# Scores first: a new order of the attention and retention work inside each slot of a hybrid decoder layer

## The reference

```
u = rms_norm(x, norm_gain);  z = u @ w_in
q_a,k_a,v_a,g_a, q_i,k_i,w_i, q_r,k_r,v_r,g_r = split(z)
# A) attention, 8 heads x 64, sparse
score[t,s] = sum_h w_i[t,h] * relu(q_i[t,h] . k_i[s]),  causal
each query keeps its 128 best keys;  p = softmax(q_a . k_a / 8 over those keys)
y_a = (p @ v_a) * silu(g_a)
# B) retention, 4 heads, qk 64, v 128, chunks of 128 tokens
S = (q_r k_r^T) * decay;  out = S @ v_r + (q_r * xi) @ state
state = state * g_chunk + (k_r * zeta)^T @ v_r
y_r = rms_norm_per_head(out) * silu(g_r)
h = x + concat(y_a, y_r) @ w_out;   result = rms_norm(h, final_gain)
```

## Time and profile before

| | us |
|---|---|
| median of 3 runs | 291.82 (291.4 to 291.87) |
| the profiled execution | 291.78 |
| its span, first to last instruction | 290.0 |
| PE busy | 280.5 |
| DVE busy | 203.1 |
| ACT busy | 142.2 |
| POOL busy | 65.5 |

### The profile page before, as it was taken

How to read it: one execution, slowest core, us unless ns; L and a number is a source line. 1 busy time by engine, 2 the same in 40 slices (tenths; PEclk the granted TensorE clock), 3 DMA queues, 4 the chain that set the end, 5 groups by cost and what they waited for, 6 DMA issues and landing times.

```text
span 290.0 us, 4405 instructions
## 1 busy us (share of the span) xinstructions
PE 280.5 (97%) x1506; PEld 239.6 (83%) x1506; DVE 203.1 (70%) x418; ACT 142.2 (49%) x303; POOL 65.5 (23%) x121
## 2 busy tenths in 40 slices
PE   7999999999999999999999999999999999999992
PEld 7996778888888788887888888888888888888892
DVE  4866779999999999999946554658635634853342
ACT  5757637525545314584368442592534662351231
POOL 1026812142200068856400103012020020000111
PEclk9999999999999999999999999999999999999998
DMA  7998404211422043152204220212200407301113
GB/s 262 407 399 299 146 3 129 82 23 60 145 73 75 4 148 88 52 145 75 75 6 138 75 72 0 84 63 73 76 0 2 145 0 241 123 36 36 75 72 146
DMA packets 13989, 30.10 MB, mean 104 GB/s; under 512 B 1168, under 2 KB 1680, under 8 KB 13968
## 3 DMA queue, kind: packets, MB, share of 16 engines
q1 hardware_dynamic: 13392, 29.04, 30.0%
q10 hardware_dynamic: 576, 0.79, 0.7%
HBM read 27.73 MB, written 2.10 MB: 103 GB/s over the span
## 4 chain that ended last, share of the span: by engine, by line
PE 61%; DVE 22%; DMA 5%; issue 4%; POOL 3%; SPq 2%; ACT 1%; POOLq 0%; DVEq 0%; ACTq 0%
PE bank L445 15%; PE bank L447 14%; PE bank L446 14%; PE bank L496 6%; DVE keys L1093 6%; DVE top L1091 5%; DMA w_raw<-in_w_in 5%; DVE w_lo L989 3%; PE bank L510 3%; DVE keys L1078 2%; PE bank L526 2%; DVE k_stack L1054 2%; PE bank L525 2%; PE bank L535 1%; PE bank L556 1%
## 5 line engine op out<-in xcount | busy, mean ns | idle before, releaser
L445 PE MATMUL bank<-w_hi,xT_hi 128*128 128x512 f32 (+1 forms) x296 | 116.6, 394 | 1.2 <-DVE w_lo L989 1.2
L447 PE MATMUL bank<-w_hi,xT_lo 128*128 128x512 f32 (+1 forms) x296 | 114.1, 385 | 0.0
L446 PE MATMUL bank<-w_lo,xT_hi 128*128 128x512 f32 (+1 forms) x296 | 113.8, 385 | 0.0
L445 PEld LDWEIGHTS bank<-w_hi,xT_hi 128*128 128x128 f32 x296 | 55.7, 188 | 12.7 <-DVE w_lo L989 2.4
L447 PEld LDWEIGHTS bank<-w_hi,xT_lo 128*128 128x128 f32 x296 | 55.6, 188 | 11.5
L446 PEld LDWEIGHTS bank<-w_lo,xT_hi 128*128 128x128 f32 x296 | 55.7, 188 | 9.8
L989 DVE TENSOR_TENSOR w_lo<-w_raw,w_hi 128x1024 fp32r<-128x1024 f32 x36 | 45.2, 1275 | 16.3 <-ACT w_hi L626 16.1
L626 ACT ACTIVATE w_hi<-w_raw 128x1024 fp32r<-128x1024 f32 x36 | 37.4, 1053 | 6.7 <-PE bank L447 3.4
L744 ACT ACTIVATE work<-work,small 128x128 f32<-128x128 f32 (+3 forms) x32 | 17.7, 555 | 31.4 <-DVE small L1116 31.3
L1091 DVE MAX8 top<-keys 128x8 f32<-128x256 f32 (+2 forms) x48 | 26.9, 559 | 1.3
L926 POOL TENSOR_TENSOR th<-zt,tab 128x64 f32<-128x64 f32 (+1 forms) x24 | 12.5, 522 | 60.6 <-ACT zt L673 57.6
(11 more groups left out here) (131 smaller groups left out, 376.7 us busy)
## 6 DMA issues: line engine op xcount, KB each, us to landing
w_raw<-in_w_in SPq DMA_DIRECT2D x28, 512.0 KB, 3.7
w_raw<-in_w_out SPq DMA_DIRECT2D x8, 512.0 KB, 3.6
retT<-in_x SPq DMA_DIRECT2D x8, 256.0 KB, 3.7
x_h<-in_first SPq DMA_DIRECT2D x2, 836.0 KB, 8.0
out<-x_h SPq DMA_DIRECT2D x4, 320.0 KB, 2.4
mix<-in_first SPq DMA_DIRECT2D x3, 418.0 KB, 4.6
v_ret<-in_x SPq DMA_DIRECT2D x2, 512.0 KB, 11.7
v_att<-in_x SPq DMA_DIRECT2D x2, 512.0 KB, 10.0
```

Source lines behind the costliest of these rows:

```text
L445: pe.matmul(o, xh, hi[:, kk, c0:c0 + w], start=first, stop=False)
L446: pe.matmul(o, xh, lo[:, kk, c0:c0 + w], start=False, stop=False)
L447: mm = pe.matmul(o, xl, hi[:, kk, c0:c0 + w], start=False, stop=last)
```

## The change

The order inside a slot is changed on three engines. On PE, `scores(s)` comes first behind the projection, then the retention work, then `values(s-2)` and `transpose_probs(s-1)`. On ACT, `probT_out(s-1)` goes from ahead of the query rounding and `exps(s)` to behind them and behind the retention squares. On DVE, `masked_max(s)` goes ahead of `gate`, `attention_out` and `decayed`. No instruction is added or taken away, and no buffer or semaphore changes.

More of the change, by code:

```diff
@@ L599, in _ @@
                 retention = RET0 <= g < RET0 + 2 * MT
-                if 0 <= g - ATT0 - 2 < STEPS:
-                    values(g - ATT0 - 2)
+                if 0 <= g - ATT0 < STEPS:
+                    scores(g - ATT0)
                 if retention and (g - RET0) % 2 == 0:
                     ret_scores((g - RET0) // 2)
[L604 to L607, removed]
                 if retention and (g - RET0) % 2:
@@ L612, in _ @@
                     ret_out(n)
+                if 0 <= g - ATT0 - 2 < STEPS:
+                    values(g - ATT0 - 2)
+                if 0 <= g - ATT0 - 1 < STEPS:
+                    transpose_probs(g - ATT0 - 1)
         @block.scalar
@@ L801, in _ @@
                     transposed_out(3)
-                if 0 <= g - ATT0 - 1 < STEPS:
-                    probT_out(g - ATT0 - 1)
                 next_block = block_split_at(g)
@@ L812, in _ @@
                     ret_squares((g - RET0) // 2)
+                if 0 <= g - ATT0 - 1 < STEPS:
+                    probT_out(g - ATT0 - 1)
                 if g >= GROUPS:
@@ L1247, in _ @@
                     mix_lo(g - (GROUPS - 1))
-                if MT * C_RG <= g < GROUPS:
-                    gate(g)
                 if g >= GROUPS:
@@ L1256, in _ @@
                     index_scores(g - MT - 1)
+                if 0 <= g - ATT0 < STEPS:
+                    masked_max(g - ATT0)
+                if MT * C_RG <= g < GROUPS:
+                    gate(g)
                 s = g - ATT0 - 2
@@ L1261, in _ @@
                     decayed((g - RET0) // 2)
-                if 0 <= g - ATT0 < STEPS:
-                    masked_max(g - ATT0)
                 if block_split_at(g) is not None:
```

## The result

The changed kernel takes 299.87 us (median of 5, 299.65 to 301.3) against 291.69: the ratio is 1.0286, 95% interval 1.0262 to 1.0309. That is 8.2 us slower, where 5.9 were forecast (297.7, range 294.4 to 300.2). The profiled execution took 299.87 us, with a span of 298.0.

The account below looks back on a forecast made before the run. PE was taken as the bound, busy 97% of the span, so every new wait is paid in full. Waits of 6.2 us (A to E plus 0.1 in slot 30) less 0.32 make +5.9: 297.7 us, range 294.4 to 300.2.

Parts of the forecast that it names:

- The second effect of PE's order: PE's tail: transposes come last, so row maxima start where the tail ends, in odd slots 1.6 us later.
- A: `ret_out(1)` in slot 27, now straight after the scores: PE waits 1.05 us for the state.
- B: `ret_scores(2)` in slot 28: PE waits 1.29 us for `retention_out(1)`.
- C: `ret_kv(2)` in the middle of slot 29: PE waits 0.62 us for `decayed(2)`.
- D: `transpose_mix(0)` in slot 31: PE waits 1.07 us for ACT's copy of step 13.
- E: `transpose_mix(1)` in slot 32: PE waits 2.07 us for ACT's copy of step 14, with four squares in between.
- The saving of 0.32 us: PE, slots 25, 27, 29, 31: one switch from plain to projection-type matmuls fewer, 4 x 0.08 = -0.32 us.
- Slots 16 to 21 at nothing: Slots 16 to 21, where DVE is full: the new order costs 0, with bounds of -0.6 to +0.6 us.
- R1: Only ACT's order counts: A to C stay hidden, D and E alone cost time; 294.6 us, chance 0.08.
- R2: Faster: no wait arises, the switch saving stays and POOL's kz is in time; 290.9 us, chance 0.03.
- R3: Nothing: waits arise, but values and transposes behind them were slack, only 0.3 is seen; 291.5 us, chance 0.04.
- R4: PE's clock grant falls to its lower level for one slot's 24 products behind the stalls; 303.3 us, chance 0.05.

Follow-up runs that it names:

- the second pair of buffers: The changed kernel with all three new orders, but odd steps write their masked scores to a second pair of buffers: 291.10 us, ratio 0.9982.

## Why the prediction was right

The time of 299.87 us lies within the range of 294.4 to 300.2, but only 0.3 us from its end. The places and causes of the waits were right; the sum was 2.3 us too small, and the bounds, made with 0.4 us for each chain, were just wide enough.

*What bounds the kernel* was right: PE's stream has no slack, and every new wait came out in the end, slot by slot.

*The second effect of PE's order*, maxima at the end of the tail, is shown by L1113's releaser and by the second pair of buffers, which removes it and with it all four new waits.

*Places A to E* are right in kind and in order. No other place of PE waits but the borderline of slot 26, slots 16 to 25 together lose nothing, and the two last `transpose_mix` are free. All of them were sized too small: by the starts 1.21, 1.48, 1.02, 1.32 and 2.47 us for A to E, and 0.40 in slot 30, against 1.05, 1.29, 0.62, 1.07, 2.07 and 0.1. (The 1.05 in the bracket at L553 equals A's number only because a bracket counts from the modelled end.) The mis-sized term is the start of the maxima. I took 0.04 and 0.16 us ahead of the slot's start, from when ACT begins to copy (0.53 us behind the transposes' start). DVE begins 0.68 behind it (191.84, 192.52), so the maxima start 0.09 to 0.10 after S with three blocks and 0.02 ahead with four: 0.13 to 0.15 more, in each slot. Behind the tail of slot 28 they start at 203.62, 0.44 after S(29), which is why slot 29 came out at 1.09 and not 0.54. The second missing term is the handing back to PE, for which I had nothing: `state` is finished at 188.59 and PE starts at 188.73; the copy is finished at 243.71 and PE starts at 243.97; it is 0.06 (`ret_kv(2)`) to 0.26 us for each wait. Over the seven waits, slot 26 with them, the first term makes 1.3 us and the second 1.05. Against them the chains from maxima to value came out shorter than worked out, by 0.11 to 0.12 us at A to C and less elsewhere, 0.4 in all. That leaves 1.97 us by which the waits are longer, of the 2.3 us that the table's two rows differ by, and it also turned the borderline of slot 26, which I set to 0, into a slot longer by 0.19. The rest I have not taken apart; a part is at the first matmuls behind a wait (L553 to L556 in slot 27 takes 0.51 us, 0.43 before).

*The saving of 0.32 us* for switches fits what the second pair shows: from S(17) to S(32) it takes 129.0 us against 129.5, with no wait gained or lost but 0.1 at kz, which leaves 0.4. It does not lie where the table's predicted row puts it: with the second pair slots 26, 28 and 30 are 0.14 to 0.18 us shorter than before, and slots 27, 29 and 31 are 0.06 to 0.08 longer.

*Slots 16 to 21 at nothing* held: S(22) is 139.07 before and 138.97 after. That S(27) is the same too is a coincidence of 0.18 us won up to S(26) and 0.19 lost in slot 26.

*The rivals.* R1 fell: A to C are there. R2 and R3 fell, and the second pair shows what R2 lacked, the buffer: with it the time is 291.10, where R2 had 290.9. R4, the clock, did not happen in the changed kernel's profile (PEclk above), through waits of 2.31 us. But in two experiments it did, behind shorter ones. The Trainium skill (TensorE: Matmul & The Clock Gate, "Part 4: PE-mode transpose") says of a transpose that "it doesn't count as PE-busy the same way". The traces can neither bear that out nor refute it, since in both falls transposes ran next to values of 64 columns and idle time.

What stays open: why the maxima of step 12 start 0.36 us later behind their transposes than all others. They do so too with ACT's order put back and with the retention output last (1.02 us behind the transposes' start in both, 1.03 here), so it is no chance of one execution. It does not hang on PE's new order or on the transposes: with DVE's order alone, where the scores release them, the maxima of step 12 start 0.56 us behind the last score matmul's start and those of steps 13 to 15 0.20. With the second pair step 12 has 0.21, like the others. And of the 0.9 us by which the profile of DVE's order put back exceeded its expectation, I have placed only a part.

## What to carry to other kernels

Moving a producer ahead gains nothing when its consumer's next instruction waits for something else, here a buffer that the last piece of the same slot still reads. Before you reorder, look for the wait that ends last, and if it is for a buffer, give that buffer a second copy first. In an in-order list the harm comes from what is put *behind* a waiting instruction: copies behind exponentials cost 2.5 us, and nothing once the exponentials did not wait. Where one engine has no idle time at all, judge a new order by the moment when each value is ready against the moment when that engine gets there, add the handover at both ends (here 0.06 to 0.26 us back to PE, and 0.13 us more from PE to DVE than I took), and expect that removing one wait can uncover the next. And when one kernel's times spread by 1% or more, compare its granted clock run by run before you explain a median: here the falls of the clock are most of the 2.6 us by which the medians made the sum of the single changes too large.

## What the runs showed of the hardware that was not expected

The clock's grant fell to 0.50 in one stretch and 0.74 and 0.86 in others, behind PE waits of 1.45 and 1.17 us and of 0.95 us, and stayed at 1.00 behind waits of 2.31 us, and in a second execution of the same kernel behind 0.96. Where it falls in some executions only, the times follow the mean granted clock: 293.19 us at 0.999 to 296.07 at 0.985 for one kernel, 297.72 at 0.999 to 300.66 at 0.985 for another. DVE takes up work from PE's transposes 0.15 us later than ACT does (0.68 against 0.53 us from the start of six of them).
